# One decoder block on one core: seven reorderings at the seams between its stages, in one change

## The reference, cut to what matters

```
h = rms_norm(x, norm_mix_pre)
z = h @ w_in                                # q 1024, k 128, v 128, u 1024, gates 2 x 2048
o_attn = sliding_window_gqa_sinks(rope(q), rope(k), v, sinks)   # 16 query heads, 2 kv heads, window 128
o_ssm  = s5_mixer(u, ...)                   # diagonal complex scan, gelu, @ w_glu, gated
y_attn, y_ssm = o_attn @ w_branch[:1024], o_ssm @ w_branch[1024:]
mixed = (sigmoid(gate_attn) * y_attn + sigmoid(gate_ssm) * y_ssm) @ w_out
x1 = x + rms_norm(mixed, norm_mix_post)
a = relu(rms_norm(x1, norm_mlp_pre) @ w_up)                     # 2048 -> 8192
out = x1 + rms_norm((a * a) @ w_down, norm_mlp_post)            # 8192 -> 2048
```

## Time and profile before

| | before |
|---|---|
| three runs | 2536.85, 2537.1, 2539.46 us, median 2537.1 |
| the profiled execution | 2539.02 us, of which the profile's span is 2537.3 us |
| PE busy | 2490.2 us (98%) |
| DVE busy | 1290.5 us (51%) |
| ACT busy | 688.7 us (27%) |
| mean granted clock of TensorE | 0.994 |

### The profile page before, as it was taken

One profiled execution on the slowest core, in us unless ns is written; L12 is line 12 of the kernel. 1 busy time (PEld: TensorE's weight loads), 2 busy tenths in 40 slices (PEclk: granted clock), 3 DMA queues, 4 the chain that ended last, 5 costly groups with the idle time before them and its releaser, 6 DMA issues.

```text
span 2537.3 us, 30565 instructions
## 1 busy us (share of the span) xinstructions
PE 2490.2 (98%) x11791; PEld 2029.7 (80%) x11791; DVE 1290.5 (51%) x1673; ACT 688.7 (27%) x935; POOL 179.5 (7%) x285
## 2 busy tenths in 40 slices
PE   7999999999999999989999999999999999999997
PEld 6866787878788888868888888888888888888886
DVE  7867588887334442364433443344344334433446
ACT  5236332333422222262221122122221221221222
POOL 1120242531000000000000000000000000000000
PEclk9999999999999999989999999999999999999999
DMA  5531334343334443343322223332333323333342
GB/s 188 138 104 42 98 113 130 113 117 117 112 99 133 149 161 129 105 161 102 106 91 92 99 99 99 99 99 83 99 101 100 95 84 99 99 99 99 99 152 97
DMA packets 84570, 279.30 MB, mean 110 GB/s; under 512 B 18208, under 2 KB 18256, under 8 KB 82576
## 3 DMA queue, kind: packets, MB, share of 16 engines
q1 hardware_dynamic: 65088, 232.81, 28.5%
q0 software_dynamic: 6880, 28.63, 3.5%
q10 hardware_dynamic: 12528, 16.83, 2.0%
HBM read 259.29 MB, written 18.94 MB: 110 GB/s over the span
## 4 chain that ended last, share of the span: by engine, by line
PE 94%; DVE 4%; DMA 1%; issue 1%; ACT 1%; POOL 0%; DVEq 0%; ACTq 0%; POOLq 0%
PE main L1513 15%; PE main L1515 14%; PE main L1514 14%; PE side L1705 6%; PE side L1703 6%; PE side L1704 6%; PE main L1705 5%; PE main L1703 5%; PE main L1704 5%; PE side L1514 5%; PE side L1515 5%; PE side L1513 5%; PE side L1556 1%; PE side L1567 1%; PE side L1648 1%
## 5 line engine op out<-in xcount | busy, mean ns | idle before, releaser
L496 ACT ACTIVATE w_hi<-w_raw 128x1024 fp32r<-128x1024 f32 x436 | 454.0, 1057 | 1092.0 <-PE main L1515 406.0
L846 DVE TENSOR_TENSOR w_lo<-w_raw,w_hi 128x1024 fp32r<-128x1024 f32 x436 | 531.8, 1237 | 388.2 <-ACT w_hi L496 369.0
L1513 PE MATMUL main<-h_hi,w_hi 128*128 128x512 f32 x1312 | 520.6, 397 | 12.7 <-DVE h_lo L864 9.5
L1515 PE MATMUL main<-h_hi,w_lo 128*128 128x512 f32 x1312 | 513.6, 391 | 0.0
L1514 PE MATMUL main<-h_lo,w_hi 128*128 128x512 f32 x1312 | 513.1, 391 | 0.0
L1513 PEld LDWEIGHTS main<-h_hi,w_hi 128*128 128x128 f32 x1312 | 248.0, 189 | 70.1 <-issue 15.4
L1515 PEld LDWEIGHTS main<-h_hi,w_lo 128*128 128x128 f32 x1312 | 247.6, 189 | 52.7
L1514 PEld LDWEIGHTS main<-h_lo,w_hi 128*128 128x128 f32 x1312 | 248.2, 189 | 49.5
L1513 PE MATMUL side<-h_hi,w_hi 128*128 128x512 f32 x512 | 199.2, 389 | 0.0
L1514 PE MATMUL side<-h_lo,w_hi 128*128 128x512 f32 x512 | 199.2, 389 | 0.0
L1515 PE MATMUL side<-h_hi,w_lo 128*128 128x512 f32 x512 | 199.2, 389 | 0.0
(11 more groups left out here) (316 smaller groups left out, 3066.1 us busy)
## 6 DMA issues: line engine op xcount, KB each, us to landing
w_raw<-wstream SPq DMA_DIRECT2D x436, 512.0 KB, 3.6
gate_scratch<-gate_stage ACTq DMA_DIRECT2D x16, 512.0 KB, 4.6
x<-x_t POOLq DMA_DIRECT2D x8, 512.0 KB, 6.8
gate_attn<-gate_scratch POOLq DMA_DIRECT2D x8, 512.0 KB, 3.8
gate_ssm<-gate_scratch POOLq DMA_DIRECT2D x8, 512.0 KB, 4.5
x_rows<-x_rows POOLq DMA_DIRECT2D x4, 1024.0 KB, 12.2
x_scratch<-x_rows ACTq DMA_DIRECT2D x4, 1024.0 KB, 4.6
x_all<-x_scratch POOLq DMA_DIRECT2D x4, 1024.0 KB, 8.2
```

Source lines behind the costliest of these rows:

```text
L496: nc.scalar.activation(WH[:, s], RAW[:, s], ACT.Copy).then_inc(hi_ready, 1)
L846: tt(WL[:, s], RAW[:, s], WH[:, s].bitcast(F32), ALU.subtract).then_inc(lo_ready, 1)
L1513: mm(o, wh, xh[:, k0 + k], start=first and k == 0, stop=False)
L1515: ins = mm(o, wl, xh[:, k0 + k], start=False, stop=last and k == 3)
```

## The change

It has seven parts.

1. The first two blocks of `w_in` are made side by side: units 0, 2, 4, 6 are the first block and 1, 3, 5, 7 the second, so that the first eight units use `x` at half the pace. The first two pieces of `x` come as single 256 KB loads on ACT's DMA queue. The parameters' load goes ahead of the rest of `x` on POOL's queue, a first small load (`cols`) behind it. Fourteen 128x128 matmuls of the constant `ones` stand ahead of the first product on PE.
2. In that stretch `time_step`, the squares and their sums are spread between the units; the S5 parameter steps start with unit 8 instead of 6, and the reciprocal norms with unit 9.
3. The products with the values are made for all four head pairs of a group at once (512 columns), behind the first quarter of the slot's unit. The buffer of transposed probabilities is laid out for it.
4. `y_hi` and `y_lo` of the first four tiles are made during the last gate units, in a place of their own; the buffers of the attention output, `m_lo` and others change places for that.
5. From `w_out` to the MLP the row blocks are handled in pairs: transposes of two row blocks side by side, splits of 256 columns, residuals of whole rows for t = 0 to 2, and the first four MLP units as two half products each (`half_product`, 256 tokens moving), the first pair's before the second pair's. All four row blocks of `x` have a buffer, and the reload of x1 goes.
6. The last norm weights are multiplied in right after each of the first two blocks, one instruction a block, inside the loop over the last units.
7. The last step of row blocks 0 to 2 works in halves of 1024 instead of quarters, with as many output DMAs.

The diff, cut to its core:

```diff
-    YH = at("y_hi", [CT, T], 48, F32R)
-    YL = at("y_lo", [CT, T], 64, F32R)
+    YH = at("y_hi", [CT, T], 144, F32R)
+    YL = at("y_lo", [CT, T], 160, F32R)
...
-    PTB = at("probs_t", [4, T], 168)
+    PTB = at("probs_t", [2, 2, 4, P], 168)
...
-    HL2 = at("h2_lo", [TT_N, KT, P], 80, F32R)
-    HH2 = at("h2_hi", [TT_N, KT, P], 144, F32R)
+    HL2 = at("h2_lo", [2, KT, 2 * P], 80, F32R)
+    HH2 = at("h2_hi", [2, KT, 2 * P], 48, F32R)
-    XR = at("x_rows", [3, D], 176)
+    XR = [at(f"x_rows{t}", [D], kib) for t, kib in enumerate((176, 184, 192, 112))]
...
+            for k in range(3):
+                pool.dma_start(tmp[k][:], params[k]).then_inc(par_landed, 16)
+            for r in range(1, KT // 2):
+                if r in (2, 3):
+                    pool.wait_ge(x_first[r - 2], 16)
+                if r >= 4:
+                    pool.wait_ge(*x_pair(r - 3))
                 pool.dma_start(XT[:, 2 * r:2 * r + 2], xT[2 * r:2 * r + 2].rearrange("k p t -> p k t")
                                ).then_inc(x_landed[r % 4], 16)
-            for k in range(3):
-                pool.dma_start(tmp[k][:], params[k]).then_inc(par_landed, 16)
+            pool.dma_start(COLS[:], cols).then_inc(cols_landed, 16)
...
-            act.dma_start(COLS[:], cols).then_inc(small_landed, 16)
+            for k in range(2):
+                act.dma_start(XT[:, k], xT[k]).then_inc(x_first[k], 16)
             unit(0, 0)
-            act.wait_ge(small_landed, 32)
-            for k in range(KT):
-                if k % 2 == 0:
-                    act.wait_ge(x_landed[k // 2 % 4], 16 * (k // 8 + 1))
-                nc.scalar.activation(HH[:, k], XT[:, k], ACT.Copy, scale=GAIN[:, 0, k:k + 1]).then_inc(xh_ready, 1)
-                if k % 4 == 3:
-                    if k < KT - 1:
-                        unit(k // 4 + 1, 0)
-            for n in range(4):
+            act.wait_ge(small_landed, 16)
...
+            h_hi(range(0, 4))
+            unit(1, 0)
+            h_hi(range(4, 8))
+            unit(2, 0)
+            unit(3, 0)
+            h_hi(range(8, 12))
+            unit(4, 0)
+            x_square(0)
+            h_hi(range(12, 16))
             unit(5, 0)
+            x_square(1)
+            unit(6, 0)
+            x_square(2)
+            unit(7, 0)
+            x_square(3)
...
+                        if g >= 1:
+                            act.wait_ge(pv_done, g)
+                        kb0 = first_key(g) // P
+                        nc.scalar.activation(PTB[:, :, kb0:2, k],
+                                             side[:, 2].rearrange("p (h b q) -> p h b q", h=2, b=2)[:, :, kb0:2],
...
+                if n in (U_GLU - 3, U_GLU - 2):
+                    act.wait_ge(c_done, CT - 1)
+                    act.wait_ge(y_ready, CT - 1)
+                    for c in range(2):
+                        y_hi(2 * (n - U_GLU + 3) + c)
...
-            act.wait_ge(unit_done, U_GLU)
+            act.wait_ge(c_done, CT)
             act.wait_ge(y_ready, CT)
-            for c in range(CT):
+            for c in range(4, CT):
...
+            def h2_hi(p, c):
+                act.wait_ge(turned, 8 * p + c + 1)
+                for i in range(2):
+                    k = 2 * c + i
+                    ins = nc.scalar.activation(HH2[:, p, k], side[:, c % 4, 2 * i * P:2 * i * P + 2 * P], ACT.Copy,
                                                scale=GAIN[:, 2, k:k + 1])
                 ins.then_inc(h2h_ready, 1)
...
+            x1_squares(0)
+            store_x1(1)
             for c in range(4):
                 h2_hi(0, c)
-            store_x1(1)
             row_scale(2)
-            for c in range(4):
+            for c in range(2):
+                unit(U_UP, c)
+                h2_hi(0, 4 + 2 * c)
+                h2_hi(0, 5 + 2 * c)
+            row_scale(3)
+            unit(U_UP, 2)
+            unit(U_UP, 3)
+            store_x1(2)
+            x1_squares(1)
+            x1_squares(2)
+            for c in range(8):
                 h2_hi(1, c)
-            unit(U_UP, 0)
-            store_x1(2)
-            row_scale(3)
-            for t, c in H2_ORDER[8:]:
-                h2_hi(t, c)
-                if (t, c) in ((3, 0), (3, 1), (3, 2)):
-                    unit(U_UP, c + 1)
             store_x1(3)
-            for t in (1, 2, 3):
-                x1_squares(t, t - 1)
+            x1_squares(3)
...
+            h_lo(range(0, 4))
+            unit(1, 0)
+            time_step(0)
+            h_lo(range(4, 8))
+            unit(2, 0)
+            time_step(1)
+            unit(3, 0)
+            h_lo(range(8, 12))
+            unit(4, 0)
+            h_lo(range(12, 16))
+            unit(5, 0)
+            x_sum(1)
+            unit(6, 0)
+            x_sum(2)
+            unit(7, 0)
+            x_sum(3)
...
-            v.wait_ge(g3_landed, 16)
-            for t in range(TT_N):
-                tt(Y[:, t, 0:2 * T], ACC[:, t, 0:2 * T], G3[:, 0:2 * T], ALU.mult)
+                    v.wait_ge(g3_landed, 16)
+                    r = slice(m * T, m * T + T)
+                    tt(Y[:, :, r], ACC[:, :, r], G3[:, r].unsqueeze(1).to_broadcast([P, TT_N, T]), ALU.mult)
...
-                for c in range(4):
-                    r = slice(c * T, c * T + T)
+                wide = 2 * T if t < TT_N - 1 else T
+                for c in range(D // wide):
+                    r = slice(c * wide, c * wide + wide)
                     stt(out=Y[:, t, r], in0=Y[:, t, r], scalar=ROW[:, 7, t:t + 1], in1=X1F[:, t, r],
...
+            pe.wait_ge(ones_set, 1)
+            for _ in range(14):
+                mm(side[:, 0, 0:P], ONES[:], ONES[:], start=True, stop=True)
+            for n in range(8):
+                b, j = n % 2, n // 2
+                product(n, n % 4, main, 2 * b, HH, HL, 4 * j, j == 0, j == 3,
+                        ready=(lambda k: pe.wait_ge(xl_ready, 4 * j + k + 1)) if b == 0 else None)
...
+                for g in group_of(slot, N_SLOT0 + 3) if k == 0 else ():
+                    n = g // 2
+                    pe.wait_ge(pt_ready, 4 * g + 4)
                     if g >= 1:
                         pe.wait_ge(o_ready, g)
-                    for b in range(2):
-                        for kb in range(first_key(g) // P, 2):
-                            ins = mm(side[HEAD * b:HEAD * b + HEAD, 3, k * P:k * P + P],
+                    for kb in range(first_key(g) // P, 2):
+                        for b in range(2):
+                            ins = mm(side[HEAD * b:HEAD * b + HEAD, 3],
                                      VTOK[:, n + kb - 1, HEAD * b:HEAD * b + HEAD],
-                                     PTB[:, a % 4, (2 * b + kb) * P:(2 * b + kb + 1) * P],
+                                     PTB[:, b, kb].rearrange("p a q -> p (a q)"),
                                      start=kb == first_key(g) // P, stop=kb == 1)
                     ins.then_inc(pv_done, 1)
...
+            def turn(p, chunks):
+                for c in chunks:
+                    for t in (2 * p, 2 * p + 1):
+                        pe.wait_ge(x1_ready, x1_count(t, 2 * c))
+                    if 8 * p + c >= 4:
+                        pe.wait_ge(h2l_ready, 8 * p + c - 3)
                     else:
                         pe.wait_ge(bank_read, B_OUT + 3)
-                    for k in range(4 * c, 4 * c + 4):
-                        ins = nc.tensor.transpose(side[:, c, (k % 4) * P:(k % 4) * P + P],
-                                                  XR[:, t % 3, k * P:k * P + P], IDENT[:])
+                    for i in range(2):
+                        k = 2 * c + i
+                        for h in range(2):
+                            ins = nc.tensor.transpose(side[:, c % 4, (2 * i + h) * P:(2 * i + h) * P + P],
+                                                      XR[2 * p + h][:, k * P:k * P + P], IDENT[:])
                     ins.then_inc(turned, 1)
...
+                        if j == 1:
+                            turn(0, (4, 5))
                     elif j == 3:
                         ins.then_inc(row_done, 1)
-                if t >= 1:
-                    turn(t - 1)
-            turn(3)
-            H2H, H2L = (x[:].rearrange("p t k j -> p k t j") for x in (HH2, HL2))
+                if t == 2:
+                    turn(0, range(4))
+            turn(0, (6, 7))
+            H2H, H2L = (x[:].rearrange("p a k j -> p k a j") for x in (HH2, HL2))
+            def half_product(p, j):
+                pe.wait_ge(lo_ready, U_UP + j + 1)
+                for k in range(4):
+                    if k % 2 == 0:
+                        pe.wait_ge(h2l_ready, 8 * p + 2 * j + k // 2 + 1)
+                    for m in range(2):
+                        wh, wl = (w[:, j % 4, k, m * P:m * P + P] for w in (WH, WL))
+                        o = main[:, m, 2 * p * P:2 * p * P + 2 * P]
+                        xh, xl = HH2[:, p, 4 * j + k], HL2[:, p, 4 * j + k]
```

(16 more changed lines are left out.)

278 lines of the change are left out of this document (132 added, 146 removed).

## The result

The changed kernel takes 2511.6 us in the median of four runs (2507.2 to 2514.3), the kernel before 2537.1 (2536.9 to 2539.5): a ratio of 0.9892, 95% interval 0.9881 to 0.9904. Four more runs, beside the first experiments, gave 2510.2. The forecast was 2506.7. The profiled execution took 2509.6 us, where the sum on record, made against the profiled execution of before, said 2508.6. The kernel before was timed again beside each of the four sets of experiments; its medians there are 2538.0, 2538.2, 2538.5 and 2538.5, so medians of different sets compare to about half a microsecond.

What follows compares the result with a forecast made beforehand. PE was taken as the bound, busy 2490.2 of 2537.3 us, so only its seams and the end could gain. Terms 8.4, 3.2, 5.8, 10.2 and 2.8 summed to 30.4, from 2537.1 to 2506.7 us; range 2499 to 2519, its own 2501 to 2512.

Steps and rivals of the forecast that it cites:

- rival (b): Seams' gains eaten by clock and DMA: start 4, MLP 8.5, attention 1.5; total gain 22.6, 2514 us; chance 0.15.
- Start: First weight units: earlier product, clock raised by the ones, fewer waits; 8.4 us gained, bounds 3 to 10.
- The first product's 1.4: Start: with x landed by 6.2, PE starts at 7.8 instead of 9.2 us, 1.4 gained.
- The clock's 2.6: Start: if the ones raise the clock by 7.8 us, twelve matmuls save 0.21 each, 2.6 us.
- Value products: Attention: one 512-column block, 1.95 us at most, saves some 0.5 a group; 3.2 us taken, bounds 0 and 4.7.
- S5 to GLU: Four tiles done early remove PE's wait for y_lo and the low clock behind it; 5.8 us, bounds 4.4 and 6.0.
- w_out to MLP: Paired row blocks, half products at 0.12 us a matmul: 10.2 us gained; bounds 13.7 and a loss of 7.
- Rival (a): Before the MLP: weight loads in the open, 0.23 us per 256-column matmul, loss of 7; total 2524 us; chance 0.09.
- Rival (d): Before the MLP: 256-column matmuls run like plain float32, 0.45 us each; slower kernel, 2567 us; chance 0.02.
- (c): w_out to MLP: second pair's chain stays late, half products only fill waits; gain 2 there, 2515 us; chance 0.05.
- End: After the last full block: merged multiplication starts rows 2.1 earlier, wider last steps 0.7; 2.8 us, bounds 0.5 and 3.2.
- signs of being wrong: A half product over 4 us, the clock falling at any seam but the MLP's, or PE waiting at unit 184.

Runs made afterwards that it cites:

- x_alone: four_orders, with the second weight unit's load sent only once the first 256 KB of x have landed: 2500.3 us against 2501.0.
- tiny_ones: four_orders, with the fourteen matmuls of ones cut from 128 to 8 columns: 2502.1 us against 2501.0.
- ones_alone: The kernel before, with only the fourteen matmuls of ones added ahead of its first product: 2544.4 us beside 2538.5.
- no_ones: four_orders without the fourteen matmuls of ones: 2532.1 us, 31 us longer.
- split_first: The changed kernel, with the second norm-weight multiplication moved behind the last two weight splits: 2507.6 us beside 2510.2.
- four_orders: The changed kernel with instructions reordered in four places (start, attention, handoff to the MLP, end): 2501.0 us.
- late_split: four_orders, with all eight tiles of the mixer's output split behind the last gate again: 2507.5 us, 6.5 more.
- narrow_values: four_orders, with each 512-column value product made as four of 128 columns in one block: 2500.8 us against 2501.0.

## Why the prediction was right, and where it was not

**The sum.** 30.4 us were forecast, 29.7 came in the trace. The median of the first four runs is 4.9 us over the forecast: 1.0 because the profiled executions differ by 29.4 and not by 30.4, and 3.9 because they lay on opposite sides, 1.9 above the median of before, 2.0 below that of after. So the median, 2511.6, ends just inside the forecast's own range (2501 to 2512) and nearer to rival (b)'s 2514 than to 2506.7; that the forecast and not (b) describes the kernel is shown by the stages, not by the total. The forecast had no term for a spread, and the change made one: waits of 2 to 3 us in the start, with the clock falling behind them or not.

**Start: 8.4 forecast, 7.75 in the first trace, 5.6 in the second.** The step that failed first is "if `x` has landed by 6.2": it landed at 7.0, since the second weight unit's 512 KB ran beside it (`x_alone` shows it: with that unit held back, `x` is there by 5.6, the product at 7.8). The 0.4 set aside for the two units was too small. The first product's 1.4 was 0.54. The clock's 2.6 (twelve times 0.21 is 2.5) held where the clock rises late without the ones: 2.4 in the trace, 2.6 at the 25th product in `tiny_ones` and at the 13th in `ones_alone`. In `no_ones` it was 1.6. That the ones last 6 us came out, but not by the columns from which the forecast had it, as the 8-column ones show. The step that failed second is the sum of squares, for which I had no term: its wait grew from 0.8 to 2.2 us, 3.0 in the other trace, because the third and fourth square each waited for the sum before. Against that, small waits of the kernel before that I had not counted went too: without its 1.4, the stretch from the 13th to the 241st product gained 6.2 where my terms for it make 4.8. No run undoes the two blocks side by side or the spread sums alone, so how the 6.2 divide between them is open.

**Value products: 3.2, measured 3.22, for partly wrong reasons.** The block took 1.87 us (198.25 to 200.12), under the 1.95 of the working, and the waits on `probs` kept their places. But I took the loop of DVE and ACT as what paces the early slots, and it is the order of the split and the mask; and behind the wait of 2.2 us the clock fell, 1.3 us, which I had not counted. Without that fall the stage would have gained some 4.5 (an estimate, 3.22 and 1.3), near my upper bound of 4.7. Two errors of opposite sign met in a right number: luck.

**S5 to GLU: 5.8, measured 6.3**, and 7.1 lost when undone from a cleaner kernel: early tiles are all of it.

**w_out to MLP: 10.2, measured 11.2.** Half products at 0.12, waits of 0.84 and 1.97 us from start to start where 1.0 and 2.0 were forecast, 30.4 us from the last row block to unit 184 where 31 were. The 0.5 set aside for the clock was not spent. Rival (a) had loads in the open, 0.23 us a matmul and a loss of 7; the trace shows 0.12. Rival (d), which needed 0.29, is out with it, and (c), which left a gain of 2 here, by the 11.2. The Trainium skill, page "TensorE: Matmul & The Clock Gate", section "Part 3: Packing small matmuls — row/col tiling", has the sentence that a weight load overlaps running matmuls only where the row group differs; the trace does not agree, since here every load takes all rows and none shows. Unit 184 was the thin cover, and held with 0.3 us. No run undoes this part, the largest term of the sum; its account rests on the two traces.

**End: 2.8, measured 1.3.** This is the step that failed in its reasoning: "The price: the last weight split is 2.3 later, so PE ends at 2525.9; DVE needs that result at 2527: hidden." The 2.1 for the merged multiplication came (DVE's rows start 30.5 us earlier, 28.4 of them from the stages before), and 0.8 for the wide last steps. But I followed only the last row. The *first* row's second half needs PE soon after the same split, and the clock, which I had left out, fell behind the wait of 3.3: 1.5 us of DVE's time. `split_first` gives these back.

**Rival (b)** came nearest in its mechanism too: some of the gain was eaten by clock and loads, in places other than those it named. It had 4 for the start, 1.5 for attention and 8.5 for the MLP, where 7.75 (5.6), 3.2 and 11.2 came. The kernel avoided the MLP's low stretch and took one in attention and one at the end.

**One of the forecast's own signs of being wrong was met.** It named a fall of the clock at any seam but the MLP's. The clock fell in attention (188.9 to 192.4 us in the first trace) and at the end (2479.3 to 2482.7), and again at both places in the second trace. What failed is the step that left the clock out of the terms for attention and the end; it cost 1.3 us in the one and, with the wait, 1.5 in the other. The other two signs of being wrong stayed away: a half product took 2.9 us, and PE did not wait at unit 184.

**What no term covered**: the fourteen matmuls of ones carry 31 us in the kernel with the four orders, of which the forecast saw 2.6; in the changed kernel itself they were not taken out. That its loop stayed loaded (50 blocks) was luck as far as the forecast goes. Had it cost the same 30 us there, the time would have been near 2541, above the kernel before and outside the range, from a cause that no rival lists.

## What to carry to other kernels

Where one engine is the bound, look for the instruction that stands ahead of the one it waits for: a handful of swaps on DVE's and ACT's queues, with four more matmuls of ones, gave 13 us here beside the 26 to 28 of the whole restructuring, and left no wait over 2 us behind the first product. A later producer is hidden only when *every* reader behind it is, the first one above all. And after any edit to the code ahead of a long loop, count the blocks on the instruction queue: if they have doubled, the change is measured together with a cost that has nothing to do with it, and a few instructions ahead of the loop can decide.

## What the runs showed of the hardware

- A few instructions more or less ahead of a loop in PE's program cost 6 or 30 us of 2500. Instructions arrive in blocks of 16384 bytes; with 50 to 52 in the run the MLP's loop stays loaded over its six turns, with 104 or 105 nine are fetched a turn, and PE stops at the turn for 0.7 to 4.8 us from start to start. The Trainium skill, "Runtime: NRT & Kernel Launch", section "Instruction fetch mechanics", says that instructions come in 16 KiB blocks, that TensorE holds 128 KiB of them, and that a taken branch whose target lies outside the current window of two pages stops the engine for a fetch. The trace agrees in the size of the blocks, and `no_ones` in the stop. It does not agree with a window of two pages: in `four_orders` a turn is 768 matmuls with as many weight loads and takes 174 us, and six turns run without a fetch or a stop. At what offset the loop falls out was not measured.
- Fourteen plain float32 matmuls of 8 columns took 6.14 us and those of 128 columns 4.9 to 6.3, with the clock risen under the wide ones only. Each is two records, and at the lower clock these start 0.21 us apart at either width.
- Whether the clock falls behind a wait is not settled by the wait's length. It fell for 3.4 us, worth 1.3 to 1.7, behind waits of 3.3 us (end) and 2.2 (`probs`) in all three traces that had them. Behind the 2.1 for `probs` it fell in `ones_alone` and not in the kernel before; behind the 4.4 at GLU for 3.4 us in the kernel before and for 6.8 in `late_split` and `ones_alone`. Behind waits of 2.0 to 3.0 in the start it fell in some traces and not in others (not behind the 2.8 of `narrow_values`), behind the stops of 3.0 and 3.3 at two turns of `no_ones` it did not, and never behind the 1.8 before the MLP. Why is open; in the start, the fourteen matmuls of ones end anywhere from 6.0 to 7.5 us.
- 256-column fp32r matmuls on all rows follow each other at 0.12 us, the weight loads fully beside them.
